# First feed-forward column pair: where a Pool wait stands, and where VectorE forms one token tile's rest

## What is computed

```
def swiglu(h, w_gate, w_up, w_down):
    return (jax.nn.silu(h @ w_gate) * (h @ w_up)) @ w_down

for layer in range(DEPTH):
    h = rmsnorm(x, mix_norm_w[layer])
    x = x + (attn_pool_mixer(h, ...) if layer % 2 == 0 else ssd_mixer(h, ...))
    h = rmsnorm(x, ffn_norm_w[layer])
    x = x + swiglu(h, w_gate[layer], w_up[layer], w_down[layer])
return rmsnorm(x, final_norm_w)
```

## Time and profile before

| | us |
|---|---|
| median of 3 runs | 2315.26 |
| lowest and highest run | 2314.67, 2315.49 |
| the profiled execution, device time | 2316.67 |
| its span in the trace | 2314.9 |
| TensorE busy | 2290.0 |
| VectorE busy | 1263.1 |
| Pool busy | 1198.0 |
| ScalarE busy | 1056.5 |

### The profile page before, as it was taken

The page is one execution under the profiler, slowest core; times in us unless marked ns, Lnnn a source line. Parts: engine busy times, 40 slices in busy tenths (PEclk is TensorE's granted clock), DMA queues, the critical chain, the costliest instruction groups (busy, mean ns, idle before and its releaser), DMA issues.

```text
span 2314.9 us, 29409 instructions
## 1 busy us (share of the span) xinstructions
PE 2290.0 (99%) x10838; PEld 1870.1 (81%) x10838; DVE 1263.1 (55%) x1657; ACT 1056.5 (46%) x1898; POOL 1198.0 (52%) x841
## 2 busy tenths in 40 slices
PE   8999999999999999999999999999999999999998
PEld 6867878888888888788888887888878888888887
DVE  7356663333436787557358347338763333336787
ACT  4046543333333446465257247238553333333445
POOL 3224288777774654223224214314388777774654
PEclk9999999999999999999999999999999999999999
DMA  5100322323228743221212212112222323227744
GB/s 161 49 25 19 119 87 87 118 87 119 88 109 292 245 147 113 57 90 48 65 56 73 71 40 91 46 55 101 101 68 106 118 87 118 87 100 281 255 147 158
DMA packets 166965, 247.92 MB, mean 107 GB/s; under 512 B 18465, under 2 KB 111533, under 8 KB 164269
## 3 DMA queue, kind: packets, MB, share of 16 engines
q1 hardware_dynamic: 162204, 233.99, 30.7%
q10 hardware_dynamic: 4624, 12.06, 1.3%
HBM read 192.93 MB, written 53.08 MB: 106 GB/s over the span
## 4 chain that ended last, share of the span: by engine, by line
PE 94%; DVE 3%; DMA 1%; issue 1%; ACT 1%; POOL 0%; SPq 0%; DVEq 0%; ACTq 0%
PE ps L1467 29%; PE ps L1469 28%; PE ps L1468 28%; PE ps L1975 1%; PE ps L1960 1%; PE ps L1967 1%; PE ps L1490 1%; PE ps L1677 1%; PE ps L1656 1%; PE ps L1940 1%; PE ps L1686 1%; PE ps L1554 0%; DVE xres L2080 0%; DMA mdec<-decay_sums 0%; DVE xn_lo L2184 0%
## 5 line engine op out<-in xcount | busy, mean ns | idle before, releaser
L746 POOL TENSOR_TENSOR w_lo<-w_raw,w_hi 128x1024 fp32r<-128x1024 f32 x74 | 176.5, 2389 | 378.8 <-ACT w_hi L922 331.4
L850 POOL TENSOR_TENSOR s_lo<-s_val,s_hi 128x512 fp32r<-128x512 f32 x154 | 234.6, 1526 | 203.0 <-ACT s_hi L1245 202.6
L2255 DVE TENSOR_TENSOR xres<-ps,xres 128x512 f32<-128x512 f32 x132 | 90.6, 688 | 412.2 <-PE ps L1469 412.2
L1467 PE MATMUL ps<-xn_hi,w_hi 128*128 128x512 f32 x784 | 310.2, 396 | 0.6 <-DVE qT L2460 0.5
L1468 PE MATMUL ps<-xn_lo,w_hi 128*128 128x512 f32 x784 | 305.4, 390 | 0.0
L1469 PE MATMUL ps<-xn_hi,w_lo 128*128 128x512 f32 x784 | 305.3, 389 | 0.0
L1467 PE MATMUL ps<-xn_hi,p_hi 128*128 128x512 f32 x704 | 274.7, 390 | 3.1 <-DVE xn_lo L2184 3.0
L1469 PE MATMUL ps<-xn_hi,p_lo 128*128 128x512 f32 x704 | 273.9, 389 | 0.0
L1468 PE MATMUL ps<-xn_lo,p_hi 128*128 128x512 f32 x704 | 273.9, 389 | 0.0
L771 POOL TENSOR_TENSOR p_lo<-p_val,p_hi 128x512 fp32r<-128x512 f32 x176 | 238.8, 1365 | 46.0 <-ACT p_hi L1057 37.5
L1057 ACT ACTIVATE p_hi<-p_val 128x512 fp32r<-128x512 f32 x176 | 111.3, 632 | 304.7 <-POOL p_val L797 304.7
(11 more groups left out here) (284 smaller groups left out, 5037.3 us busy)
## 6 DMA issues: line engine op xcount, KB each, us to landing
s_val<-hidden SPq DMA_DIRECT2D x154, 256.0 KB, 2.8
hidden<-xres SPq DMA_DIRECT2D x20, 1792.0 KB, 6.4
wv_g<-in_w_gate SPq DMA_DIRECT2D x22, 1024.0 KB, 5.1
wv_u<-in_w_up SPq DMA_DIRECT2D x20, 1024.0 KB, 5.1
w_raw<-in_ssd_w_in SPq DMA_DIRECT2D x40, 512.0 KB, 3.9
d_val<-in_w_down SPq DMA_DIRECT2D x70, 256.0 KB, 3.9
rows_v<-in_w_down SPq DMA_DIRECT2D x64, 256.0 KB, 3.5
mdec<-decay_sums SPq DMA_DIRECT2D x32, 512.0 KB, 3.9
```

Of the source, the lines that this page charges most:

```text
L746: pool.tensor_tensor(w_lo[piece.slot][:, :], raw[piece.raw][:, :], f(w_hi[piece.slot][:, :]), ALU.subtract).then_inc(lo_done, 1)
L850: pool.tensor_tensor(s_lo[i][:, :], s_val[i][:, :], f(s_hi[i][:, :]), ALU.subtract)\
L1467: pe.matmul(dst, l_hi, r_hi, start=first, stop=False, skip_group_check=reopened)
L2255: dve.tensor_tensor(tmp, bank, tmp, ALU.add).then_inc(c_ready, 1)
```

## The change

Two edits, each acting once in each of the two layers' feed-forward blocks.

1. On Pool, the wait for VectorE's T2 rest of tile 3 stands ahead of the rest of M3g. It stood behind it, ahead of the rest of M7g.
2. On VectorE, the T1 rest of tile 1 stands behind T1, T2, T3 and the B22 rest of tile 2. It stood ahead of them. The list of counts follows: B22 of tile 2 is now finished before T1 of tile 1.

```diff
@@ -416,7 +416,7 @@
-        comb_lo_order = Order([("B22", 0), ("T1", 0), ("T2", 0), ("B22", 1), ("T1", 1), ("B22", 2),
+        comb_lo_order = Order([("B22", 0), ("T1", 0), ("T2", 0), ("B22", 1), ("B22", 2), ("T1", 1),
@@ -815,8 +815,8 @@
                 p_lo_of(0, "M6g")
+                pool.wait_ge(comb_lo_done, comb_lo_order.count(layer, "T2", 3))
                 p_lo_of(0, "M3g")
-                pool.wait_ge(comb_lo_done, comb_lo_order.count(layer, "T2", 3))
                 p_lo_of(0, "M7g")
@@ -2224,11 +2224,11 @@
                 make(7)
-                tail_lo1(1)
                 tail_t1(2)
                 tail_t2(2)
                 tail_t3(2)
                 tail_b22(2)
+                tail_lo1(1)
                 tail_t1(3)
```

## The result

The changed kernel is slower: 2318.86 us in the median of 22 runs (2316.68 to 2321.98) against 2315.7 of the kernel before (22 runs, 2314.67 to 2317.53) on the same chip, a ratio of 1.0013 with the interval 1.0007 to 1.0018. That is 3.2 us, about 0.14%. The forecast was 2314.7 with a range up to 2316.2, so both its sign and its range are wrong, though the time is within the 0.2% to which most of the chance had gone. The profiled execution took 2320.85 us.

A forecast was written before the change was run, and what follows sets the result against it. TensorE was taken as the bound, busy 2290.0 of 2314.9 us, with at most 5.3 us to regain. A net 0.31 us in each layer, 0.6 in all, off the median 2315.26 gave 2314.7, range 2312.0 to 2316.2.

The forecast's parts named there:

- the one on covers: Behind M6u, layer 0: M4g's rest and the next gate-weight load come 0.6 us later, but M1g, 10.9 us on, is not reached.
- Removing T1's collision: VectorE's T1 rest of tile 3 meets no Pool operation: 0.60 instead of 1.69 us, M5g 1.11 earlier per layer.
- The step with the near tie: Pool takes M6g's rest at 289.92, 0.11 us ahead of VectorE's T1 rest of tile 1, so edit 2 gives 0.
- The rival in which VectorE wins that tie: VectorE's T1 rest of tile 1 goes before Pool's M6g rest: 1.4 us a layer, 2312.5 us; chance 0.13.
- The price on Pool: Pool's line from M3g's to M6u's rest lasts 11.60 us instead of 9.90, so M6u's rest is ready at 310.04.
- The thinnest cover, that of M5u's rest: Pool ends M5u's rest at 306.65 against 306.75 wanted; worth 0.1 us if gone.
- The net gain: Per layer, M6u's start with the slower product behind idle time counted: 0.31 us, 0.6 us for both layers.
- The tie at the first T4 rest: VectorE's first T4 rest goes before Pool's M5u rest, as at 305.92 before; Pool winning would shorten its line by 0.55 us.
- the rival drawn from a computed lead of 0.01: Pool wins at VectorE's first T4 rest: 0.9 us a layer, 1.8 in both, 2313.5 us; chance 0.12.
- The slower rival: Pool's line grows but VectorE's T2 rest of tile 3 stays at 298.79: 1.6 us lost in both layers, 2316.9; chance 0.10.
- The slower end of the range: 2316.2 us, taking in the forecast, the run-to-run spread and part of the slower case of 2316.9.

## Why the prediction was wrong

**The step that failed** is the one on covers: "The rest of M4g comes at 311.7 instead of 311.16, and with it the load of the next gate weights, 0.6 later; the first product that needs them, M1g of the second pair, starts four products behind M6u, 10.9 us on, and is not reached. Behind M6u TensorE's order is unchanged and everything shifts with it." The delay of 0.6 was right (0.62 measured). Two things were not looked at. The cover was taken at the first consumer on TensorE, but the chain runs through ScalarE, which needed the weights 0.3 us after they landed and takes its work in order, then through Pool, which has no idle time there to take a delay back, and then through ScalarE's queue again to a copy that reads only a finished product and had 0.5 us. And the load's duration was taken as fixed, while it grew by 1.3 us. With the delay alone, the copy would hardly have stopped TensorE: in layer 1, where the load did not grow, M3g starts 0.1 to 0.4 us late in the changed kernel, its repeat and the run with the wait alone. The issue, 0.95 late against TensorE, the growth (1.3) and Pool's further collisions (1.1), less ScalarE's cover (0.3) and the copy's (0.5), make the 2.5, and in the execution shown the clock added 1.5. The growth is the largest of these terms, and its own cause stays open, as said above.

**Removing T1's collision.** The gain was as forecast: M5g starts 1.09 us earlier against M2u (computed 1.11), the wait before M5g is 0.41 (forecast 0.4), that before M6g 0.58 (0.56).

**Edit 2.** The step with the near tie held: Pool took M6g 0.08 ahead of VectorE (computed 0.11), and the order alone moved nothing. The rival in which VectorE wins that tie fell.

**The price on Pool.** Its size held: from M3g's rest at 299.02 to the end of M6u's at 310.62 it lasts 11.60, as computed. The thinnest cover, that of M5u's rest, ran out: M5u starts 0.07 late, and M6u 0.56 more, 0.63 together, where 0.68 was computed. The wait listed before M6u is 0.38 and not 0.5 to 0.7, because idle time counts from the end of the last record (0.39 long) and not from the start that was due, 0.23 behind it. The net gain, forecast 0.31 in a layer, was 0.33 and 0.42; between the two kernels with the cut load it is 0.31 and 0.39, so 0.70 for both, where 0.6 stood.

**The tie at the first T4 rest.** VectorE won it, as forecast, in both layers. The recorded starts don't say why: in layer 0 of the changed kernel VectorE's is 0.004 us ahead (305.403 against 305.407), in layer 1 Pool's is, by 0.006 (1700.524 against 1700.530), and in the kernel before Pool's is, by 0.004 and 0.009. The rule of the Trainium skill ("SBUF — State Buffer", section "SBUF: two separate sides") is that the one of the two engines that starts first holds the shared port pair. Where the starts lie 0.03 us or more apart (and 0.08 at M6g's rest) the rows agree with it. Within 0.01 the recorded starts don't decide it: at this rest VectorE passed first in both layers of all ten profiled kernels, and in 18 of the 20 Pool's record starts first. So the forecast that VectorE wins was right by its rows, and the rival drawn from a computed lead of 0.01 had no ground in them.

**The slower rival** put the loss at the wrong place: it wanted a shift that did not come, and the shift came in full (1.09). The slower end of the range was drawn from it, so nothing in the range stood for a transfer that comes late.

## What to carry to other kernels

When an edit moves the release of a buffer, follow the load to the first engine that touches it, and from there down each in-order queue to the next point that TensorE needs, whether or not the work at that point reads the data: the thinnest cover on that way is the one that counts. Engines that are nearly full on the way hand a delay on whole, and may add to it. Here a gain of 0.7 us was not worth a load of 1 MB issued 0.6 us later; cutting the load in two with an early first half took the dependence away here.

## What was not expected of the hardware

A load of 1 MB took 5.2 to 5.4 us in the three kernels that issued it at 310.8 to 311.2, and 6.5 or 6.6 in the five that issued it 0.4 to 1.5 us behind the kernel before; the difference is a tail at 23 to 24 GB/s, the pace of one of 16 DMA engines, in every run in which the fetch of 16 KB of instructions (0.9 to 1.3 us for its packet) fell into the middle of the load. And the idle stretches of 2.5 to 2.7 us of TensorE were each followed, at once or some matmuls on, by about seven matmuls 0.43 us apart (granted clock 0.59 over 4 us in the changed kernel), which adds 1.5 us to the wait, in the four profiled executions that have such a stretch, while those of 1.28, 1.50 and 1.59 us were not. By the mean granted clock of the unprofiled runs it may not follow in each of them.

A near tie of VectorE and Pool is not even. Among operations of these two kinds in the ten traces in which one held up the other, VectorE passed first in 53 of the 55 whose recorded starts lie within 0.01 us, Pool's up to 0.01 ahead included; with Pool's record 0.03 us or more ahead, Pool passed first in every one.
